# Recurrences with each head's rows issued one step sooner and three memory tiles moved, and six layer norms whose mean is made of a summed tile and one more

## What is computed

```python
def _layer_norm(x, g, b):
    mu = jnp.mean(xf, -1, keepdims=True)
    xc = xf - mu
    var = jnp.mean(xc * xc, -1, keepdims=True)
    return xc * lax.rsqrt(var + LN_EPS) * g + b
...
# mLSTM (SSD alike, with its own decay): per head, scores times a decay, times the values
scores = jnp.einsum("bhctk,bhcsk->bhcts", qc, kc) * jnp.exp(dmat - m_row[..., None])
num = ... + jnp.einsum("bhcts,bhcsv->bhctv", scores, vc)
...
mkv = (mem @ w_mem_kv).reshape(B, M, 2, MX_HEADS, MX_HEAD_DIM)   # for each of the two layers
```

## Time and profile before

| what | value |
|---|---|
| median of 3 runs | 3602.48 us (3598.13 to 3613.75) |
| profiled execution: its own time | 3599.84 us |
| profiled execution: its span | 3598.0 us |
| busy: PE, DVE, ACT, POOL | 95%, 69%, 53%, 6% of the span |
| mean granted clock of PE | 0.964 of full |
| recurrences, m loop to the end of the stage | 391.8 to 522.4 us from the span's start |
| the six means | within 551.7 to 585.6, 1819.1 to 1853.6, and from 2293.6 on |

### The profile page before, as it was taken

One profiled execution on the slowest core, in us unless ns is written; L12 is line 12 of the kernel. 1 busy time (PEld: TensorE's weight loads), 2 busy tenths in 40 slices (PEclk: granted clock), 3 DMA queues, 4 the chain that ended last, 5 costly groups with the idle time before them and its releaser, 6 DMA issues. The chain is left out here.

```text
span 3598.0 us, 45290 instructions
## 1 busy us (share of the span) xinstructions
PE 3414.2 (95%) x16920; PEld 2725.5 (76%) x16920; DVE 2468.8 (69%) x2833; ACT 1903.2 (53%) x2144; POOL 209.2 (6%) x202
## 2 busy tenths in 40 slices
PE   8998977999999999999989998999999999899998
PEld 7886555788888888888758886778887877678886
DVE  6554454999999999999748766466525775546642
ACT  4213233778787777777636536254415535534422
POOL 0000000111112111111100000000000000000000
PEclk9988888999999999999999999999999999999999
DMA  4111124999999999999712110132321111123331
GB/s 150 45 30 34 55 98 167 352 373 363 371 362 368 366 372 364 370 362 367 291 39 83 59 59 28 49 100 94 105 89 65 64 58 56 28 78 98 96 101 64
DMA packets 118801, 600.27 MB, mean 167 GB/s; under 512 B 20722, under 2 KB 24194, under 8 KB 68130
## 3 DMA queue, kind: packets, MB, share of 16 engines
q1 hardware_dynamic: 105346, 580.93, 44.5%
q0 software_dynamic: 13312, 17.35, 2.0%
HBM read 586.06 MB, written 28.90 MB: 171 GB/s over the span
## 5 line engine op out<-in xcount | busy, mean ns | idle before, releaser
L2326 DVE TENSOR_TENSOR wl<-raw,wh 128x2048 fp32r<-128x2048 f32 x384 | 872.9, 2287 | 54.4 <-ACT wh L2256 53.3
L2256 ACT ACTIVATE wh<-raw 128x2048 fp32r<-128x2048 f32 x384 | 735.7, 1916 | 191.3 <-PE pu L2201 143.2
L2199 PE MATMUL pu<-wh,Xh 128*128 128x512 f32 x1024 | 410.0, 400 | 0.0
L2200 PE MATMUL pu<-wl,Xh 128*128 128x512 f32 x1024 | 399.9, 391 | 0.0
L2201 PE MATMUL pu<-wh,Xl 128*128 128x512 f32 x1024 | 399.8, 390 | 0.0
L4061 ACT ACTIVATE w_high<-w_raw 128x1024 fp32r<-128x1024 f32 (+1 forms) x120 | 137.1, 1146 | 334.3 <-PE acc L4035 172.0
L4094 DVE TENSOR_TENSOR w_low<-w_raw,w_high 128x1024 fp32r<-128x1024 f32 (+1 forms) x120 | 159.6, 1331 | 199.0 <-PE ps L3993 107.7
L4017 PE MATMUL ps<-x_high,w_high 128*128 128x512 f32 x656 | 255.2, 389 | 0.0
L4018 PE MATMUL ps<-x_low,w_high 128*128 128x512 f32 x656 | 255.2, 389 | 0.0
L2199 PEld LDWEIGHTS pu<-wh,Xh 128*128 128x128 f32 x1024 | 192.7, 188 | 45.7 <-issue 8.1
L2201 PEld LDWEIGHTS pu<-wh,Xl 128*128 128x128 f32 x1024 | 192.6, 188 | 42.4
(11 more groups left out here) (720 smaller groups left out, 6803.6 us busy)
## 6 DMA issues: line engine op xcount, KB each, us to landing
raw<-in_exp_w SPq DMA_DIRECT2D x384, 1024.0 KB, 7.7
w_raw<-in_w_in SPq DMA_DIRECT2D x100, 512.0 KB, 3.4
w_raw<-in_w_up SPq DMA_DIRECT2D x88, 512.0 KB, 3.8
w_raw<-in_w_down SPq DMA_DIRECT2D x32, 704.0 KB, 4.0
w_raw<-in_w_out SPq DMA_DIRECT2D x32, 384.0 KB, 3.1
kv_raw<-in_w_mem_kv SPq DMA_DIRECT2D x16, 512.0 KB, 3.8
x<-in_x SPq DMA_DIRECT2D x4, 1024.0 KB, 7.6
w_raw<-in_w_out SPq DMA_DIRECT2D x8, 512.0 KB, 4.4
```

Source lines behind the costliest of these rows:

```text
L2199: nc.tensor.matmul(o, lh[:, k, :], wh[:, m % PARTS, c], start=(m >= 8 and kh == 0 and kk == 0), stop=False)
L2200: nc.tensor.matmul(o, lh[:, k, :], wl[:, m % PARTS, c], start=False, stop=False)
L2256: nc.scalar.activation(wh[:, m % PARTS, :], raw[:, m % RAW, :], ACT.Copy).then_inc(w_high, 1)
L2326: nc.vector.tensor_tensor(wl[:, m % PARTS, :], raw[:, m % RAW, :], wh[:, m % PARTS, :], ALU.subtract).then_inc(w_low, 1)
```

## The change

It does three things, and adds no transfer.

- **Rows one step sooner.** `m_rows(h + 1)` and `s_rows(h + 1)` are issued behind the sums of the third step of a head and no longer ahead of the sums of the fourth one.
- **Three memory tiles.** Tile 7 is issued whole ahead of `m_sums(0)`, tile 14 whole behind `s_sums(15)`, and tile 15 whole behind the sums of squares. The takes on ScalarE follow. VectorE no longer waits for the last memory product ahead of `ys`. For this the second buffer of low parts gets another place, and tile 15 another bank.
- **Six means.** VectorE adds up tiles 0 to 6 of `x` as they are made (`add_to_sum`, six additions of 128x512 a norm). TensorE multiplies that sum once (`mean_of_sum`) and tile 7 once (`mean_part`), where it did eight products.

```diff
@@ -375,6 +375,19 @@
...
+    def mean_of_sum(self, pe, total, summed):
+
+        pe.wait_ge(summed, DT - 2)
+        self.K.nc.tensor.matmul(self.mu, self.K.c("mean1024"), total, start=True, stop=False)
+
+    def add_to_sum(self, dve, total, j, made, summed):
+
+        if 1 <= j < DT - 1:
+            dve.wait_ge(made, j + 1)
+            if j >= 2:
+                dve.wait_ge(summed, j - 1)
+            self.K.nc.vector.tensor_tensor(total, self.x[:, 0, :] if j == 1 else total, self.x[:, j, :], ALU.add).then_inc(summed, 1)
...
@@ -612,6 +625,8 @@
...
+        with ExitStack() as held:
+            memory.wl.append(K.sb(held, "kv_low1", [P, D], F32R))
...
@@ -638,7 +653,7 @@
...
-        kv_bank = lambda t: B[:, (1 if t < MEM_TILES or t == 9 or t == 11 else 2 if t in (13, 15) else 7), 0:MEM]
+        kv_bank = lambda t: B[:, (1 if t < MEM_TILES or t == 9 or t == 11 else 2 if t == 13 else 3 if t == 15 else 7), 0:MEM]
...
@@ -811,13 +826,14 @@
...
                     if n + 1 < LAST:
                         m_score(n + 1)
-                    if n % NT == NT - 1 and n + 1 < LAST:
-                        m_rows(n // NT + 1)
                     if n == 2 * NT:
                         pe.wait_ge(memory.taken, MEM_TILES)
+                    if n == 0:
+                        for half in (0, 1):
+                            memory.tensor(pe, MEM_TILES - 1, half, kv_bank(MEM_TILES - 1))
                     m_sums(n)
-                    if n in (2, 3):
-                        memory.tensor(pe, MEM_TILES - 1, n % 2, kv_bank(MEM_TILES - 1))
+                    if n % NT == NT - 2 and n + 2 < LAST:
+                        m_rows(n // NT + 1)
...
@@ -837,9 +853,9 @@
...
-                    if n % NT == NT - 1 and n + 1 < LAST:
+                    s_sums(n)
+                    if n % NT == NT - 2 and n + 2 < LAST:
                         s_rows(n // NT + 1)
-                    s_sums(n)
...
@@ -856,19 +872,24 @@
...
-                    memory.tensor(pe, t, n % 2, kv_bank(t))
+                    if n < 12:
+                        memory.tensor(pe, t, n % 2, kv_bank(t))
                     if n == 12:
                         pe.wait_ge(m_inverse, 1)
                         head_spread(B[:, 1, :], 0).then_inc(m_spread, 1)
                         head_spread(B[:, 0, :], 1).then_inc(m_spread, 1)
+                for half in (0, 1):
+                    memory.tensor(pe, memory.count - 2, half, kv_bank(memory.count - 2))
                 pe.wait_ge(s_exponent, LAST)
                 for t in range(2):
                     pe.wait_ge(s_squared, t + 1)
                     mm = quarter_sums(B[:, 6, 0:P], K.c("mean256")[:, 0:32], t, t == 0, t == 1)
                 mm.then_inc(s_var, 1)
+                for half in (0, 1):
+                    memory.tensor(pe, memory.count - 1, half, kv_bank(memory.count - 1))
                 pe.wait_ge(s_inverse, 1)
...
-                pe.wait_ge(memory.taken, memory.count)
+                pe.wait_ge(memory.taken, memory.count - 1)
...
@@ -947,7 +968,7 @@
...
-                    if n == 5:
+                    if n == 1:
                         memory.scalar_take(act, MEM_TILES - 1, kv_bank(MEM_TILES - 1))
                         memory.scalar_high(act, MEM_TILES + 1)
...
@@ -959,7 +980,7 @@
...
-                    if n >= 3 and n % 2:
+                    if 3 <= n < 15 and n % 2:
                         t = MEM_TILES + (n - 3) // 2
...
@@ -974,14 +995,15 @@
...
-                memory.scalar_take(act, memory.count - 1, kv_bank(memory.count - 1))
                 act.wait_ge(s_gated, 1)
                 act.wait_ge(m_var, 1)
                 for t in range(2):
                     nc.scalar.activation(sq[:, t, :], ys[:, t, :], ACT.Square).then_inc(s_squared, 1)
+                memory.scalar_take(act, memory.count - 2, kv_bank(memory.count - 2))
                 act.wait_ge(s_var, 1)
                 act.wait_ge(m_spread, 2)
                 nc.scalar.activation(root[:, 0, :], B[:, 6, 0:P], ACT.Sqrt, bias=K.c("eps", P, 0, 1)).then_inc(s_root, 1)
+                memory.scalar_take(act, memory.count - 1, kv_bank(memory.count - 1))
...
@@ -1179,7 +1201,6 @@
...
-                dve.wait_ge(memory.product, memory.count)
...
@@ -1884,16 +1906,11 @@
...
-                def mean(t):
-                    pe.wait_ge(taken, t + 1)
-                    return norm.mean_part(t)
-
                 for n in range(DT):
                     tile(n)
-                    if n >= 2:
-                        mean(n - 2)
-                mean(DT - 2)
-                mean(DT - 1).then_inc(norm.mean_ready, 1)
+                norm.mean_of_sum(pe, total_x[:, :], x_summed)
+                pe.wait_ge(taken, DT)
+                norm.mean_part(DT - 1).then_inc(norm.mean_ready, 1)
...
@@ -1971,6 +1988,7 @@
...
+                    norm.add_to_sum(dve, total_x[:, :], n, taken, x_summed)
...
         for n in range(DT):
             tile(n)
-            if n >= 2:
-                mean(n - 2)
-        mean(DT - 2)
-        mean(DT - 1).then_inc(norm.mean_ready, 1)
+        norm.mean_of_sum(pe, self.e[:, 0, :], self.summed)
+        pe.wait_ge(self.embedded, DT)
+        norm.mean_part(DT - 1).then_inc(norm.mean_ready, 1)
...
+            self.norm.add_to_sum(dve, self.e[:, 0, :], n, self.embedded, self.summed)
...
                     for i in range(4, len(OUT_UNITS)):
+                        if i == len(OUT_UNITS) - 1:
+                            norm.mean_of_sum(pe, dv[:, 0, :], x_summed)
                         out_unit(i)
-                        if OUT_UNITS[i - 1][1]:
-                            out_mean(OUT_UNITS[i - 1][0])
-                    out_mean(DT - 1)
+                    pe.wait_ge(w_taken, DT)
+                    norm.mean_part(DT - 1)
...
+                            norm.add_to_sum(dve, dv[:, 0, :], OUT_UNITS[i - 1][0], w_taken, x_summed)
...
                 for t in range(DT):
                     down(t, 0)
-                    if t:
-                        mean(t - 1)
+                    if t == DT - 1:
+                        norm.mean_of_sum(pe, total[:, :], summed)
                     down(t, 1)
-                mean(DT - 1)
+                pe.wait_ge(taken, DT)
+                norm.mean_part(DT - 1)
...
+                        norm.add_to_sum(dve, total[:, :], t - 1, taken, summed)
```

More of the change, by code:

```diff
@@ L1817, in arrival @@
         one = K.sb(ctx, "onehot", [P, NT, TOP_K, EXPERTS])
+        total_x = K.sb(ctx, "x_sum", [P, S])
         acc = K.ps(ctx, "acc", [P, 2, S])
@@ L1825, in arrival @@
             "parts", "parts_taken", "router_in", "b_in", "b_split_h", "b_split_l", "zeroed", "stored", "y_split_h", "y_split_l", "w_split_h", "w_split_l", "product",
-            "taken", "own", "logits", "shifted", "exps", "turned", "tokens", "x_in0", "x_in1"]
+            "taken", "own", "logits", "shifted", "exps", "turned", "tokens", "x_in0", "x_in1", "x_summed"]
         with stage(nc, *names, *NORM_SEMS) as (block, *sems):
@@ L1829, in arrival @@
             (parts, parts_taken, router_in, b_in, b_split_h, b_split_l, zeroed, stored, y_split_h, y_split_l, w_split_h, w_split_l, product,
-             taken, own, logits, shifted, exps, turned, tokens, x_in0, x_in1) = sems[3:len(names)]
+             taken, own, logits, shifted, exps, turned, tokens, x_in0, x_in1, x_summed) = sems[3:len(names)]
             norm = Norm(K, x, gain, bias, mu[:, :], spare[:, :], lambda j: sq[:, j, :], root[:, :], sems[len(names):])
@@ L2556 @@
     "p_in", "v_in", "p_split_h", "p_split_l", "v_split_h", "v_split_l", "e_made", "e_taken", "y_turned", "y_added", "x_split_h", "x_split_l",
-    "w_split_h", "w_split_l", "product", "gate", "weighed", "embedded"]
+    "w_split_h", "w_split_l", "product", "gate", "weighed", "embedded", "e_summed"]
 PT = PLE // P
@@ L2584, in __init__ @@
         (self.p_in, self.v_in, self.p_split_h, self.p_split_l, self.v_split_h, self.v_split_l, self.e_made, self.e_taken, self.turned, self.added,
-         self.x_split_h, self.x_split_l, self.w_split_h, self.w_split_l, self.product, self.gate, self.weighed, self.embedded) = sems[NT + 3:n]
+         self.x_split_h, self.x_split_l, self.w_split_h, self.w_split_l, self.product, self.gate, self.weighed, self.embedded, self.summed) = sems[NT + 3:n]
         self.norm = Norm(K, x, gain, bias, mu, spare, lambda j: yt[:, j // 2, (j % 2) * S:(j % 2) * S + S], root[:, :], sems[n:])
@@ L2646, in tile @@
             mm.then_inc(self.product, 1)
-        def mean(t):
-            pe.wait_ge(self.embedded, t + 1)
-            return norm.mean_part(t)
         for t in range(DT):
@@ L2747, in first_block @@
         c1 = ctx.enter_context(ExitStack())
-        with ExitStack() as held:
-            kv_low1 = K.sb(held, "kv_low1", [P, D], F32R)
         y = K.sb(c1, "y", [P, DT, S])
@@ L2767, in first_block @@
             memory = MemoryTiles(K, a, y[:, 4:8, :].rearrange("p t (a m) -> p (t a) m", m=MEM), [kv_raw0, kv_raw1], [kv_high0, kv_high1],
```

(13 more changed lines are left out.)

3 lines of the change are left out of this document (1 added, 2 removed).

## The result

| what | before | changed |
|---|---|---|
| median of 4 runs each, on one chip | 3600.56 us (3598.13 to 3613.75) | 3557.32 us (3550.02 to 3560.52) |
| ratio, with its 95% interval | | 0.9874 [0.9853, 0.9895] |
| profiled execution: own time, span | 3599.84, 3598.0 | 3560.52, 3558.9 |
| mean granted clock of PE | 0.964 | 0.963 |

The kernel is 1.3% faster; 3549 was forecast, with 3538 to 3566 as the range. The profiled execution is the slowest of its four, and its 3560.5 us lie in the second case, that of a clock that falls again.

What follows compares the result with a forecast made beforehand. TensorE, at work for nearly the whole span, was taken as the bound. 3599.8 less 31.0 for the means and 20.5 for the recurrences gave 3548.3; the forecast was 3549 us, range 3538 to 3566.

Steps and rivals of the forecast that it cites:

- the second case: Recurrences: the clock falls again at the shorter waits, they give 11 us or less; 3558 to 3566 us, chance 0.23.
- The six means: Six norms: 36 of 48 mean products go, 31.0 us gained with 28 as lower end; the additions cost no path.
- Rivals 3 to 5: Means give nothing, 3579 to 3588 us (0.07); VectorE becomes the bound, 3590 to 3604 (0.02); late addition, over 3618 (0.03).
- The s loop: Tiles leave, head-change waits shrink, some clock returns and VectorE limits next: gain 7 to 12.4 us, taken as 10.
- `ys` sooner and the end: End of the stage: `ys` starts 1.7 us sooner; tiles 14 and 15 placed there cost 1.2 us.
- the 3 us later: End of the stage, sign of a wrong prediction: the spread comes more than 3 us later behind the squares than before.
- The m loop: Shorter head-change waits, tile 7 moved and clock regained: 5.5 us if the clock falls as before, 14 if never; taken 10.
- The head changes' term of waiting: M loop: the score runs inside the wait at three head changes, leaving 0.3 us of each; gain 3.2 us.
- The term of tile 7: M loop: tile 7, 3.3 us at full clock, fits in the first wait of 3.4 us; gain 3.3 us.
- a sign of being wrong: M loop: the prediction is wrong if tile 7 is still running when the first sums could start.
- The step that failed is the third: M loop's clock term: of 11.8 us shortfall, about 9 would come back if no wait set the clock down.
- the cases: Whole kernel: both parts pay as worked out, 3541 to 3557 us, chance 0.65; or the clock falls again, 3558 to 3566, 0.23.

Runs made afterwards that it cites:

- experiment 10: The kernel before with VectorE's six additions a norm added and TensorE still making eight mean products: 3601.77 us, ratio 1.0005.
- experiment 6: The kernel before with the m loop's rows products of heads two to four over 128 partitions, not 4: 3592.80 us, m loop 51.91.

## Why the prediction held, and where it was off

- **The six means: right.** 31.0 us forecast; 31.7 by the run with the means alone, within 23 to 40. The profiles say it more closely: from the stage's end to the reciprocal of the last norm it is 3056.8 to 3066.4 us in the seven with the old means and 3026.2 to 3034.8 in the seven with the new ones, 30.6 on average. The parts can be read one by one. In the first `feed_forward`, from the last group of products of the first unit to that of the sixteenth, 2602.78 to 2722.40 became 2579.90 to 2694.06: 5.46 us less, for 5.35. From norm to norm the two `feed_forward` are 6.0 and 5.8 us shorter on average, which is 0.5 more than the products account for, and no run says where that comes from. From the first product of `Embedding`'s output part to its last mean it was 51.86 us and is 47.41, 47.39 and 47.37: 4.5 for 4.5. `arrival`, from its stage's start to its norm, took 62.3 to 66.8 us in the seven profiles with the old means and 57.4 to 59.7 in the seven with the new ones, 6.1 on average for 5.3; the stretch wanders too much to say more. Rivals 3 to 5 are out: experiment 10 shows the additions free, and no wait stands ahead of the sum's product.
- **The s loop: right.** 10 forecast, 9.4, 9.9 and 9.8 measured. Its waits stayed nearly as long in total (4.7 and 4.5 us), and what went is TensorE's busy time, 52.9 to 43.9 us. The tiles account for 4.9 us of it. The clock rose from 0.85 to 0.93, and to 0.96 in the two later profiles, so by (1 - clock) x length the loss to it fell from 8.7 us to 3.4 and 1.9, an estimate. So here the clock did come back. VectorE, busy for 40.1 of the 48.6 us, is the one waited for, as forecast.
- **`ys` sooner and the end: right within about 1 us.** +1.7 and -1.2 were forecast, 0.5 together, and the end is 1.0, 1.0 and 1.8 us shorter. From the first rows to the next stage it is 13.8, 22.8 and 18.9 us less, for 20.5. The spread stands 3.55 us behind the squares, where it was 3.10, far from the 3 us later that would have spoken against the forecast.
- **The m loop: the mis-sized term.** Forecast 10 of 5.5 to 14; measured 3.4, 12.0 and 7.3, 7.6 on average. The old loop wanders as well, with 58.8, 55.7 and 58.8 us in three profiles; against its mean the gain is 6.6. The head changes' term of waiting was right: 1.37 fell to 0.31. The term of tile 7 was right in what left the loop, but its cover was short. The prediction had named a tile 7 that still runs when the first sums could start as a sign of being wrong, and it came: 1.2 us, in all three profiles. The first sums then ran at the full clock, which made up for it. The step that failed is the third: "about 9 would come back" if no wait set the clock down, and "I take 10, as the waits that stay are short". The wait was taken for what sets the clock down, since each slow stretch stood behind one. The counts show that at this place the shortened wait changed next to nothing (10 of 12 for 8 of 9). What does decide the falls stays open. The rows product, which the sentence names last and prices at nothing, is one candidate by its size and another by its place: moved once more it had 0 of 6, but the last waits went with it. The lower end of 5.5 was too high as well. It kept the loss to the clock as it was, but the loop lost more to it in the first profile: the granted clock of 0.88, 0.77 and 0.73 behind the three head changes became 0.75, 0.75 and 0.65.
- **The second case** was given 0.23. By the clock it came true in the profiled execution, whose recurrences gave 13.8 us, a little over its 11, and whose time is in its 3558 to 3566. In the later two it is half true. The median near 3557 lies between the cases, because one kernel meets several clocks. That 3557 still falls into the range owes something to its width: it holds both cases. The chances were put on cases where they belonged on a distribution within one.
- **The rule behind that case.** The Trainium skill, "TensorE: Matmul & The Clock Gate", section "A second HAM failure mode: psum-queue depth-cycling", says of another kernel that short idles between groups of products, frequent enough, made the clock oscillate. The changed kernel agrees, with falls behind waits of 0.31 us. The run of experiment 6 does not, with three waits of 1.37 us and 1.00 behind each, while its repeat fell behind two of three. The rule names what can happen, and in this loop not how often.
- **The first profile against the forecast.** It missed 3548.3 by 12.2 us. 6.7 of them are the recurrences (13.8 for 20.5). The rest is 5.4 of the norms' 31.0: from the stage's end to the reciprocal of the last norm 25.6 us were saved in it. Against the average of all seven old profiles it would be 28.6, so a part of the 5.4 is that this stretch was short in the profile of before. Unchanged stretches there move by as much from one execution to the next; that from `arrival`'s norm to that of `Embedding` took 1268.5 us before, and 1272 to 1276 in five profiles with that part unchanged.

## What to carry to other kernels

Work that the critical engine does between units, with nobody waiting, is worth its full duration when it goes to an engine with slack: count the products, multiply, and check that the last addition has cover. What comes back from the clock is no such term. Price a wait by its own length, and put the clock's share into the range, not into the sum, until several profiles of one kernel show how often it falls: in the s loop it came back, in the m loop behind 2 of 12 head changes. Before filling a wait, reckon the filling at the low clock too; tile 7 took 4.2 us there and not 3.3. One profile of a stage with a clock that comes and goes says little: here the same loop took 46.8, 51.5 and 55.4 us.

## What the runs showed of the hardware

- A product over 4 partitions takes as long as one over 128: 1.12 us both, at 512 columns in plain fp32. The Trainium skill, "TensorE: Matmul & The Clock Gate", section "Why this matters for your kernels", says the like of 32 partitions, and the trace agrees. In what came behind them the two differ by count, 23 of 27 head changes below the full clock with 4 partitions and 2 of 9 with 128. The chips differ too, and the runs do not part the two.
- A fall needs no new long wait. In the changed kernel it began right behind one of 0.31 us (the sums at 408.61 took 0.57 us for 0.38, the score of 384 columns at 409.11 took 1.64 for 0.91). In the second profile the clock fell at this first head change too. At the second one, where the first profile fell again behind 0.32 us (1.65 us for the score at 422.54), the same instructions stood behind 0.32 us and stayed at the full clock.
- A small change of order went with the clock of the whole loop. With the rows behind the third step's sums the parts behind the head changes had the full clock in 2 of 12 cases, and with the rows ahead of them in 6 of 6, on two chips. Whether the last 0.3 us of waiting or the neighbour of the product does it is open.
- Where the clock stayed full, VectorE became the one waited for: 0.70 us ahead of the 512-column sums at 417.37 in the changed kernel's second profile. With the rows ahead of the third sums even that wait is gone, and TensorE is at work for 42.55 of the loop's 43.45 us.
